# Last down pair of a hybrid decoder's FFN in token chunks of 352 and 176 columns, with the last sums, spreads and stores in another order

## What is computed

```python
h2 = rmsnorm(x, norm2_w)
gu = h2 @ w_ffn_up
x = x + ((silu(gu[..., :D_FF]) * gu[..., D_FF:]) @ w_ffn_down)
...
def rmsnorm(x, w):
    y = x * lax.rsqrt(jnp.mean(x * x, axis=-1, keepdims=True) + EPS)
    return y * w
y_prompt, y_sample = rmsnorm(xp, final_norm_w), rmsnorm(xs, final_norm_w)
```

## Time and profile before

| | us |
|---|---|
| median of 3 runs | 1695.5 (1695.05 to 1696.23) |
| the profiled execution's own device time | 1691.98 |
| its span, first to last instruction | 1690.3 |
| PE busy in the span | 1654.9 (98%) |
| DVE / ACT / POOL busy | 963.9 / 555.4 / 797.7 |

### The profile page before, as it was taken

One profiled execution on the slowest core, in us unless ns is written; L12 is line 12 of the kernel. 1 busy time (PEld: TensorE's weight loads), 2 busy tenths in 40 slices (PEclk: granted clock), 3 DMA queues, 4 the chain that ended last, 5 costly groups with the idle time before them and its releaser, 6 DMA issues. The chain is left out here.

```text
span 1690.3 us, 30914 instructions
## 1 busy us (share of the span) xinstructions
PE 1654.9 (98%) x12241; PEld 1606.1 (95%) x12241; DVE 963.9 (57%) x1634; ACT 555.4 (33%) x1240; POOL 797.7 (47%) x764
## 2 busy tenths in 40 slices
PE   7999999999999999999999998999999999999997
PEld 7999999999999998888999988999999999999997
DVE  6859811406535454777882379666666555744346
ACT  5332121342113232544320144434444333322233
POOL 5483122222222121231422245777777777787774
PEclk9999999999999999999999999999999999999998
DMA  5364362232323245334454441434333344966443
GB/s 208 84 127 135 103 207 90 91 90 90 95 84 102 88 135 165 123 128 141 144 199 150 152 150 39 185 146 154 146 148 140 141 166 162 362 231 261 164 188 103
DMA packets 95661, 245.86 MB, mean 145 GB/s; under 512 B 14352, under 2 KB 42000, under 8 KB 95272
## 3 DMA queue, kind: packets, MB, share of 16 engines
q1 hardware_dynamic: 73392, 174.08, 30.1%
q0 software_dynamic: 10256, 33.59, 6.4%
q10 hardware_dynamic: 11880, 36.36, 6.3%
HBM read 177.11 MB, written 66.65 MB: 144 GB/s over the span
## 5 line engine op out<-in xcount | busy, mean ns | idle before, releaser
L1627 PE MATMUL ps<-HL,WH 128*128 128x384 f32 (+1 forms) x1536 | 507.5, 330 | 5.1 <-DVE HL L689 1.8
L1628 PE MATMUL ps<-HH,WL 128*128 128x384 f32 (+1 forms) x1536 | 496.9, 324 | 0.0
L1629 PE MATMUL ps<-HH,WH 128*128 128x384 f32 (+1 forms) x1536 | 496.0, 323 | 0.0
L1627 PEld LDWEIGHTS ps<-HL,WH 128*128 128x128 f32 x1536 | 289.2, 188 | 16.5 <-issue 10.1
L1628 PEld LDWEIGHTS ps<-HH,WL 128*128 128x128 f32 x1536 | 289.5, 188 | 0.3
L1629 PEld LDWEIGHTS ps<-HH,WH 128*128 128x128 f32 x1536 | 289.3, 188 | 0.0
L1270 POOL TENSOR_TENSOR WL<-WRAW,WH 128x1024 fp32r<-128x1024 f32 x59 | 144.7, 2452 | 230.6 <-DMA WH<-in_w 230.6
L1267 POOL DMA_DIRECT2D WH<-in_w x59 | 34.5, 585 | 365.6 <-PE ps L1629 364.1
L2918 DVE TENSOR_TENSOR X<-X,ps 128x528 f32<-128x528 f32 (+2 forms) x170 | 107.9, 656 | 155.7 <-PE ps L2222 104.7
L2311 ACT ACTIVATE GT<-ps 128x384 f32<-128x384 f32 (+1 forms) x72 | 33.3, 464 | 214.1 <-PE ps L1629 189.2
L2918 DVE TENSOR_TENSOR RB<-RB,ps 128x528 f32<-128x528 f32 x60 | 42.1, 701 | 107.9 <-ACT RB L2833 89.2
(11 more groups left out here) (468 smaller groups left out, 4271.4 us busy)
## 6 DMA issues: line engine op xcount, KB each, us to landing
WRAW<-in_w SPq DMA_DIRECT2D x75, 512.0 KB, 3.4
ffn_scratch<-STG SPq DMA_DIRECT2D x70, 528.0 KB, 3.0
WH<-in_w POOLq DMA_DIRECT2D x62, 512.0 KB, 4.3
SOP<-ffn_scratch SPq DMA_DIRECT2D x36, 528.0 KB, 8.0
gate_scratch<-GT ACTq DMA_DIRECT2D x24, 528.0 KB, 3.4
PX<-gate_scratch ACTq DMA_DIRECT2D x22, 528.0 KB, 4.1
HL<-ffn_scratch SPq DMA_DIRECT2D x22, 528.0 KB, 10.7
RAWB<-in_w SPq DMA_DIRECT2D x10, 1024.0 KB, 6.1
```

What stands on the lines that cost most here:

```text
L1627: nc.tensor.matmul(out, wh, rl, start=start, stop=False)
L1628: nc.tensor.matmul(out, wl, rh, start=False, stop=False)
L1629: return nc.tensor.matmul(out, wh, rh, start=False, stop=stop)
```

## The change

The chunks of the last pair become 352 and 176 columns (`LAST_COLS`). Groups 0 and 1 now have 352 columns (four blocks of 88), groups 2 and 3 have 176 (two blocks). Product 1's add on DVE becomes two instructions, one for each chunk. On PE, `final_sums(1)` and both spreads of groups 0 and 1 move to other places between the products, and the sums of group 3 go ahead of the spread of group 2. On ACT both roots come ahead of both copies. On DVE the rows of groups 0 and 1 move behind and between the adds of chunk 1. Of group 3's stores ACT now issues two.

```diff
+LAST_COLS = ((0, 352), (352, 176))
-        t0 = (HALF, 0)[g % 2] + CHUNK * (g // 2)
-        return slice(t0, t0 + CHUNK)
+        t0, w = LAST_COLS[g // 2]
+        t0 += (HALF, 0)[g % 2]
+        return slice(t0, t0 + w)
...
-                if (g, rows) != (GROUPS - 1, OUT_ROWS[0]):
+                if g < GROUPS - 1 or rows == OUT_ROWS[2]:
...
         final_sums(0)
         last_product(1, 7)
-        final_spread(0)
         final_sums(1)
         last_product(1, 6)
+        final_spread(0)
+        last_product(1, 4)
         final_spread(1)
-        for product in LAST_CHUNK[3:]:
+        for product in LAST_CHUNK[4:]:
             last_product(1, product)
         final_sums(2)
+        final_sums(3)
         final_spread(2)
-        final_sums(3)
         final_spread(3)
...
             if c == 0:
                 final_root(0)
+                final_root(1)
                 spread_copy(0)
-                final_root(1)
                 spread_copy(1)
+        final_root(2)
+        final_root(3)
         spread_copy(2)
-        final_root(3)
         spread_copy(3)
-        rows_done(act, GROUPS - 1, *OUT_ROWS[0])
-        out_dma(*group_out(GROUPS - 1, *OUT_ROWS[0]))
+        for rows in OUT_ROWS[0:2]:
+            rows_done(act, GROUPS - 1, *rows)
+            out_dma(*group_out(GROUPS - 1, *rows))
...
-        down_add(LAST, 3, 0, 0, 1)
+        after(dve, pd, done_count(LAST, 1))
+        for c, (t0, w) in enumerate(LAST_COLS):
+            a = down_quadrant(3, 0, 0)[:, t0:t0 + w]
+            tt(a, a, last_quad(1, c), ALU.add).then_inc(dd.sem, 1)
...
         group_square_sum(1, 7)
+        last_down_add(1, 5, 1, 1)
         group_square_sum(1, 6)
+        last_down_add(1, 7, 1, 1, 1)
         final_recip(0)
-        last_down_add(1, 5, 1, 1)
-        final_rows(0, (3, 4))
-        final_recip(1)
-        final_rows(0, (5,))
-        last_down_add(1, 7, 1, 1, 1)
-        final_rows(0, (6, 7))
-        final_rows(1, (3, 4))
         last_down_add(1, 6, 1, 1, 2)
         last_down_add(1, 6, 1, 0)
+        final_recip(1)
         last_down_add(1, 6, 0, 1)
+        final_rows(0, (3, 4))
+        last_down_add(1, 4, 1, 0, 4)
         group_square_sum(2, 7)
-        last_down_add(1, 4, 1, 0, 4)
+        final_rows(0, (5,))
         last_down_add(1, 3, 0, 1, 5)
+        final_rows(0, (6, 7))
         group_square_sum(2, 6)
         last_down_add(1, 2, 0, 0)
+        final_rows(1, (3,))
         group_square_sum(3, 7)
+        final_rows(1, (4,))
+        group_square_sum(3, 6)
         final_recip(2)
-        group_square_sum(3, 6)
-        final_rows(1, (5, 6, 7))
-        final_rows(2, (3, 4))
+        final_rows(1, (5,))
         final_recip(3)
-        final_rows(2, (5, 6, 7))
+        final_rows(1, (6, 7))
+        final_rows(2, range(3, KD))
         final_rows(3, range(3, KD))
```

More of the change, by code:

```diff
@@ L853, in group_cols, with group_width @@
     def group_cols(g):
-        t0 = (HALF, 0)[g % 2] + CHUNK * (g // 2)
-        return slice(t0, t0 + CHUNK)
+        t0, w = LAST_COLS[g // 2]
+        t0 += (HALF, 0)[g % 2]
+        return slice(t0, t0 + w)
+    def group_width(g):
+        return LAST_COLS[g // 2][1]
     def group_bank(g):
@@ L862, in group_sums @@
     def group_sums(g):
-        return group_bank(g)[0:TOKENS, 496:499]
+        return group_bank(g)[0:TOKENS, 496:496 + group_width(g) // TOKENS]
     def group_roots(g):
-        return RC2[0:TOKENS, 3 * g:3 * g + 3]
+        return RC2[0:TOKENS, (0, 4, 8, 10)[g]:(0, 4, 8, 10)[g] + group_width(g) // TOKENS]
     def last_part(c, product):
@@ L872, in last_add @@
     def last_add(c, n):
-        return 9 * (LAST - UP_PAIRS) + 1 + 8 * c + n
+        return 9 * (LAST - UP_PAIRS) + 2 + 8 * c + n
     OUT_ROWS = [(0, 3), (3, 6), (6, 8)]
@@ L952, in quad, with last_quad @@
         return ps_all[:, QUAD[product]:QUAD[product] + 2, 0:CHUNK]
+    def last_quad(product, c):
+        return bank[QUAD[product] + c][:, 0:LAST_COLS[c][1]]
     def by_chunk(a):
@@ L976, in moving @@
         cols = slice(CHUNK * c, CHUNK * c + CHUNK)
+        if x == LAST:
+            cols = slice(LAST_COLS[c][0], sum(LAST_COLS[c]))
         if x >= UP_PAIRS:
@@ L2215, in product_chunk @@
             high, lo = ring(7 * x + i)
-            out = quad(product)[:, c, :]
+            out = last_quad(product, c) if x == LAST else quad(product)[:, c, :]
             for k in range(nk):
@@ L2248, in final_sums @@
             t0 = group_cols(g).start
-            for b in range(3):
+            for b in range(group_width(g) // TOKENS):
                 last = nc.tensor.matmul(group_sums(g)[:, b:b + 1], AC5[:, t0 + TOKENS * b:t0 + TOKENS * (b + 1)], prm("ones", 0, 1),
@@ L2880, in spread_copy @@
             after(act, fspr, g + 1)
-            nc.scalar.copy(SPREAD[:, group_cols(g)], group_bank(g)[:, 0:CHUNK]).then_inc(sc_ok, 1)
+            nc.scalar.copy(SPREAD[:, group_cols(g)], group_bank(g)[:, 0:group_width(g)]).then_inc(sc_ok, 1)
         after(act, fad, 5)
@@ L2888, in _ @@
             final_square(7, l, GT, last_add(c, 7))
-            if c == 1:
-                final_root(2)
             final_square(6, l, SQ5, last_add(c, 8))
@@ L2893, in _ @@
                 final_root(0)
+                final_root(1)
                 spread_copy(0)
-                final_root(1)
                 spread_copy(1)
+        final_root(2)
+        final_root(3)
         spread_copy(2)
-        final_root(3)
         spread_copy(3)
-        rows_done(act, GROUPS - 1, *OUT_ROWS[0])
-        out_dma(*group_out(GROUPS - 1, *OUT_ROWS[0]))
-        assert outs[0] + 11 == N_OUT_TOTAL
+        for rows in OUT_ROWS[0:2]:
+            rows_done(act, GROUPS - 1, *rows)
+            out_dma(*group_out(GROUPS - 1, *rows))
+        assert outs[0] + 10 == N_OUT_TOTAL
     @block.vector
@@ L3539, in last_down_add @@
                 after(dve, dd, last_add(c, turn))
-            a = down_quadrant(3, t, n)[:, CHUNK * c:CHUNK * c + CHUNK]
-            tt(a, a, quad(product)[:, c, :], ALU.add).then_inc(dd.sem, 1)
+            t0, w = LAST_COLS[c]
+            a = down_quadrant(3, t, n)[:, t0:t0 + w]
+            tt(a, a, last_quad(product, c), ALU.add).then_inc(dd.sem, 1)
         def group_square_sum(g, k):
@@ L3559, in final_rows @@
                 row = X1[:, k, group_cols(g)]
-                stt(row, row, prm("normf", k, 1), group_bank(g)[:, 0:CHUNK], ALU.mult, ALU.mult).then_inc(y_ok, 1)
+                stt(row, row, prm("normf", k, 1), group_bank(g)[:, 0:group_width(g)], ALU.mult, ALU.mult).then_inc(y_ok, 1)
         for x in range(UP_PAIRS, PAIRS):
```

## The result

The changed kernel took 1696.36 us (median of 20; 1695.23 to 1701.38), the kernel before in the same session 1693.85 (median of 20). The ratio is **1.0017, 95% interval 1.0011 to 1.0023**: some 2.5 to 2.9 us slower. That is under the 0.2% that was set as the bound of "the same", but with twenty runs of each the interval leaves out 1, so the loss can be told from no change. The forecast was +2.2 us and 0.13%, so it held.

A forecast was written before the change was run, and what follows sets the result against it. The stores' DMA rate bounds the tail: end is first byte plus 12.53 us of DMA, gaps and 1.57 us. First byte +4.9 and gaps -2.75 give +2.2 on the 1695.5 median: 1697.7 us, range 1695.5 to 1699.8.

The forecast's parts named there:

- Widths on PE: Last pair's matmuls on PE: 352 columns cost 0.161 us each, 176 columns 0.111, held up by the weight load.
- Only columns count: Rival for PE's narrow matmuls: 0.081 us each, without a weight-load floor; -1.1 us, 1696.6 us; chance 0.17.
- loads not hidden: Rival for PE's narrow matmuls: load and stream add up to 0.19 us each; +2.9 us, 1700.6 us; chance 0.15.
- The path to the first store: Work in the last pair up to the first byte of `y`: that byte comes 4.9 us later.
- The gaps: Pauses between the tail's stretches of stores: none left, so -2.75 us.
- 12.53 unchanged: DMA time of all twelve stores in the tail: stays 12.53 us, as pieces and bytes stay the same in number.
- 1.57 us from the last byte to the end: Close of the tail: the span ends a constant 1.57 us after the stores' last byte.
- The sum: Whole tail: first byte +4.9 us and gaps -2.75 us make +2.2 us.
- Two queues: 0: Group 3's stores: ACT's second store saves only SP's issue time behind a full DMA queue; 0 us.
- Sums ahead of spreads in the last groups: 0: Groups 2 and 3: sums before spread order work finished 1 us and more before its store is wanted; 0 us.
- the cover that was named: In the tail: the store queue itself hides the reordered work of groups 2 and 3.
- The compute chain as the bound: Rival for the tail: computing the last row sets the end; -0.7 us, 1694.8 us; chance 0.05.

The follow-up runs named there:

- e1: The changed kernel with both chunks of the last pair at 264 columns, its new order and store queues kept; ratio 1.0003 to the kernel before.
- e7: The kernel before with early orders for groups 0 and 1 and 100 wait instructions at the start of PE's program; ratio 0.9992 to the kernel before.
- e9: The changed kernel with 60 wait instructions on PE ahead of the first pair of the up projections; ratio 1.0041 to the kernel before.
- e3: The changed kernel with one store of group 3 on ACT's queue, the second back on SP's; ratio 1.0020 to the kernel before.
- e2: The kernel before with chunks of 352 and 176 columns alone, its orders and store queues kept; ratio 1.0009 to the kernel before.
- e12: The kernel before with only sums of groups 2 and 3 ahead of group 2's spread, both roots ahead of both copies; ratio 1.0007 to the kernel before.
- e5: The changed kernel with 100 wait instructions at the very start of PE's program; ratio 1.0035 to the kernel before.
- e11: The kernel before with three more operations on a dead buffer at the end of POOL's program; ratio 1.0008 to the kernel before.
- e8: The kernel before with chunks of 352 and 176, early orders and 100 wait instructions at the start of PE's program; ratio 1.0017 to the kernel before.

## Why the prediction was right, point by point

- **Widths on PE: right.** 0.161 and 0.111 were taken, 0.162 and 0.111 stand in the rows. The floor at the weight load, for which one distant row of 32 columns was the evidence, is there. *Only columns count* (0.081) and *loads not hidden* (0.19) are out. The Trainium skill's figure (TensorE: Matmul & The Clock Gate, section LDWEIGHTS), by which a load of 128 columns takes 107 ns, agrees with the 0.111.
- **The path to the first store: right.** To group 0's sums +2.04 was worked out; from the mark it is 13.13 us against 11.08, +2.05. The spread ends 0.2 us earlier than forecast, POOL starts at 1677.52 - 3.16 = 1674.36 on the old scale (forecast 1674.5), and its three rows take 2.7, not 2.88. First byte: +4.6 for +4.9.
- **The gaps: the mechanism right, the gain too large.** One solid stretch without a gap, as forecast. But "12.53 unchanged" was the step that failed: from first to last byte it is 13.9 us, 15.5 before, so 1.6 were won and not 2.75. The sum had no term for the program code. A gap isn't all loss: in the kernel before, the 16 KB of code were fetched in one. In e1 the packet lay among the stores at 1681.02, some engine still moved bytes in the gap that followed, and the last stretch ended with less than 0.2 us of a lone one. The gap of e1:

```profile
1684.40:1685.60 1.20, 0.00 (x0) 0.00 (x0) 1.20 (x4) 0.00 (x0) 1.20 (x3) 0.50 0.10 33
```

  Packed tight, the stores of the changed kernel end with a lone stretch. With the code ahead of the stores the time from first to last byte is 0.9 (e7) and 1.0 us (e9) shorter, most of the 1.1 that was missing. The two packets of the changed kernel, 0.88 and 0.35 us, make 1.23, so they aren't the whole account either way, and e9's remaining 0.65 us stays open.
- **1.57 us from the last byte to the end: wrong as a constant.** In the kernel before the end waited for POOL (28.4 + 5.6), not for the stores, whose last byte plus 0.97 would have ended it 0.4 us earlier. The prediction read the chain of the earlier trace rows to its 0.94 us of issue and took what starts then for the queue of the stores. It is POOL's own queue of instructions (POOLq), and behind it come POOL's last two rows:

```profile
1682.49 0.77 POOLq L3652
1683.27 1.40 POOL X L1295 x2
```

  These end at 1684.67, 5.62 us ahead of the end, and by the chain no DMA comes behind them. It isn't proof by itself, since the chain follows the last instruction and knows no stores: the changed kernel's ends on POOL too, 6.5 us ahead of an end that the stores set. There 0.99 us follow the last byte: 0.4 us back.
- **The sum:** +4.6 - 1.6 - 0.4 = +2.6, forecast +4.9 - 2.75 + 0 = +2.2. The errors, -0.3, +1.1 and -0.4, nearly cancelled. That the total came so close is luck: two terms were wrong in opposite directions. What is no luck is the mechanism: the first byte was delayed as worked out, and the gaps closed.
- **Two queues: 0**, as far as the times of e3 tell (within some 2 us), and with the lone stretch in e2 too. **Sums ahead of spreads in the last groups: 0**, not tried alone in the changed kernel; its solid stretch of stores fits the cover that was named, and e12 shows 0.5 us where that queue isn't full.
- **The compute chain as the bound**, a rival at 0.05, did not come: but it was worked out without POOL's 5.6 us, and it is nearer than it looked. POOL's limit in the changed kernel is 30.1 + 5.6 = 35.7, 0.9 under its end; e9 runs into it.
- **Left out of it altogether: the clock.** In two of four profiles of this order with uneven chunks (e3, e5; not in the changed kernel and e9) it fell to 0.5 about 16 us behind the mark, with PE busy nearly all the time ahead of it (3.20 of 3.30 us in e3's row), and the tail took 39 us. No profile of another kernel here has it that early. The rows of PE ahead of it look alike with and without, so why it falls is open. The changed kernel's times reach to 1701.4, those of before to 1696.6: some of its executions may be such, which no run shows.

The difference of 3.16 us ahead of the last pair has its rows too. The same 6.9 us of the changed kernel and of before:

```profile
1055.40:1062.30 6.90, 5.91 (x27) 5.91 (x28) 6.08 (x8) 2.33 (x4) 2.99 (x2) 0.51 0.98 304
```

```profile
1053.50:1057.00 3.50, 3.04 (x14) 3.04 (x15) 2.80 (x5) 2.10 (x4) 0.68 (x1) 0.51 0.97 240
1057.00:1062.30 5.30, 5.30 (x45) 5.30 (x45) 4.03 (x5) 1.38 (x3) 2.93 (x3) 1.00 1.00 400
```

Such stretches at half clock came and went between executions whose instructions up to there are the same. Ahead of the mark they make 13.7 us in the changed kernel's profile and 3.4 in that of before. By the two rows of e9 and the changed kernel above, 3.4 us of it cost PE 12 of 30 matmuls, 1.4 us: as much as most of the kernels here differ by.

## What to carry to other kernels

Ahead of a sum over the last stretch, list what the end of the program can wait for, each with its own constant, and see from several profiles which one holds: here the two limits, of the last store and of POOL's last instruction, stood 0.4 us apart. A gap between transfers that looks like waste may hold work of its own (here program code and late pieces of stores), so closing it can give back less than its length. Compare tails from a mark inside the program, since executions drift by more than such a change is worth.

## What the runs showed of the hardware

- The span ended 5.61 to 5.66 us after POOL's last instruction in eleven of the fourteen profiles, and never sooner; three more operations on POOL moved the end by their 1.8 us (e11). Why the drain takes so long was not tried.
- Program code competes with stores: 16 KB per 256 PE instructions came as one packet of 0.88 to 1.63 us beside the stores, and with it ahead of them the stores were 0.9 to 1.0 us shorter (e7, e9).
- 200 waits on PE that were long satisfied, two to an instruction, moved PE's first matmul by 4.7 to 4.8 us; 120 in the middle of the program took PE 1.3 us beyond the wait that should have hidden them.
- A square sum of 176 columns on DVE that started inside one of POOL's final rows ended 0.2 us after that row. One that started with POOL's row took its usual 0.33 us, and POOL's row took 1.12 instead of 0.93. The changed kernel has both, DVE and POOL:

```profile
1679.62 0.82 DVE L2929 TENSOR_TENSOR AC<-AC,GT 128x176 f32<-128x176 f32 x1 [0.83 <-ACT GT L2864]
1679.31 0.93 POOL L1305 TENSOR_TENSOR X<-X,SPREAD 128x352 f32<-128x352 f32 x1
...
1682.08 0.33 DVE L2929 TENSOR_TENSOR AC<-AC,SQ 128x176 f32<-128x176 f32 x1
1682.08 1.12 POOL L1305 TENSOR_TENSOR X<-X,SPREAD 128x352 f32<-128x352 f32 x1
```

  e3, e8 and e9 each have one of the first kind too (0.93, 0.96 and 0.82 us), and all three end 0.2 us after POOL's row.
